# A two-block fp32 network on one core: the second block's attention loop reordered, and products of constants put in front of TensorE's waits

## The reference, cut to what matters

```python
for layer in range(DEPTH):                       # 2
    h = modulate(rmsnorm(x, norm_g[layer, 0]), sh1, sc1)
    x = x + 0.5 * g1 * swiglu_2(h, ...)          # feed-forward, FFN_C
    h = modulate(rmsnorm(x, norm_g[layer, 1]), sh2, sc2)
    proj = h @ w_in[layer]                       # the Z tiles
    (qa, ka, va, qb, kb, vb, qi, ki, wi, qc, kc, vc) = jnp.split(proj, ...)
    ...
    oa = moba_attention(qa, ka, ...)             # 4 heads, causal softmax here (256 tokens, one block)
    ob = dsa_attention(qb, kb, ..., qi, ki, wi)  # 4 heads, softmax over the picked keys
    oc = stick_breaking_attention(qc, kc, vc)    # 8 heads: logs, a running sum, an exponential
    o = rms_per_head(concat([oa, ob, oc])) * out_g[layer]
    x = x + g2 * (o @ w_out[layer])              # the Z_O tiles
    h = modulate(rmsnorm(x, norm_g[layer, 2]), sh3, sc3)
    x = x + 0.5 * g3 * swiglu_2(h, ...)          # feed-forward, FFN_D
```

## Time and profile before

| what | value |
| --- | --- |
| median of three runs | 2839.84 us (2837.78 to 2842.38) |
| the profiled execution, its own time | 2839.58 us |
| span from its first to its last instruction | 2837.5 us |
| PE busy | 2766.8 us, 98% of the span |
| DVE busy | 1951.3 us, 69% |
| ACT busy | 1366.8 us, 48% |
| mean granted TensorE clock | 0.992 |
| DMA | 564.42 MB, mean 199 GB/s |

### The profile page before, as it was taken

The page is one execution under the profiler, slowest core; times in us unless marked ns, Lnnn a source line. Parts: engine busy times, 40 slices in busy tenths (PEclk is TensorE's granted clock), DMA queues, the critical chain, the costliest instruction groups (busy, mean ns, idle before and its releaser), DMA issues.

```text
span 2837.5 us, 37822 instructions
## 1 busy us (share of the span) xinstructions
PE 2766.8 (98%) x16120; PEld 2426.8 (86%) x16120; DVE 1951.3 (69%) x2187; ACT 1366.8 (48%) x1562; POOL 228.7 (8%) x201
## 2 busy tenths in 40 slices
PE   8999999999999999999999999999899999999999
PEld 6889999998888889999998887878878878788787
DVE  6668876655666678877655667677876676677644
ACT  5444545455444445545454444444644444446433
POOL 0000420000000000520000000003000000030000
PEclk9999999999999999999999999999999999998999
DMA  8655433445766655333446666653266676442454
GB/s 306 257 220 183 149 125 136 164 164 210 263 261 248 248 208 189 138 136 132 171 165 228 257 255 243 260 218 134 90 244 251 239 274 253 177 150 95 176 189 148
DMA packets 82038, 564.42 MB, mean 199 GB/s; under 512 B 9072, under 2 KB 10576, under 8 KB 15952
## 3 DMA queue, kind: packets, MB, share of 16 engines
q1 hardware_dynamic: 66272, 465.47, 44.8%
q0 software_dynamic: 15600, 96.55, 9.0%
HBM read 560.86 MB, written 1.12 MB: 198 GB/s over the span
## 4 chain that ended last, share of the span: by engine, by line
PE 78%; DVE 13%; ACT 4%; POOL 2%; issue 2%; DMA 1%; SPq 0%; POOLq 0%; ACTq 0%; DVEq 0%
PE ps L332 71%; DVE ring_lo L327 4%; ACT w_hi L320 2%; POOL qk L2038 1%; PE ps L899 1%; POOL rope_a L2034 1%; DVE a_hg L1806 1%; DMA rows<-mod_rows 1%; DMA ring<-stream 1%; DVE e L1786 1%; DVE e L1785 1%; PE ps L1287 1%; DVE h_lo L576 0%; PE ps L1416 0%; PE ps L1442 0%
## 5 line engine op out<-in xcount | busy, mean ns | idle before, releaser
L327 DVE TENSOR_TENSOR ring_lo<-ring,w_hi 128x2048 fp32r<-128x2048 f32 x422 | 973.8, 2310 | 484.0 <-ACT w_hi L320 473.0
L320 ACT ACTIVATE w_hi<-ring 128x2048 fp32r<-128x2048 f32 x422 | 806.4, 1911 | 318.6 <-PE ps L332 188.0
L332 PE MATMUL ps<-w_hi,h_hi 128*128 128x512 f32 (+1 forms) x1920 | 728.9, 380 | 18.1 <-DVE ring_lo L327 9.0
L332 PE MATMUL ps<-w_hi,h_lo 128*128 128x512 f32 (+1 forms) x1920 | 717.0, 373 | 0.0
L332 PE MATMUL ps<-ring_lo,h_hi 128*128 128x512 f32 (+1 forms) x1920 | 716.3, 373 | 0.0
L332 PEld LDWEIGHTS ps<-w_hi,h_hi 128*128 128x128 f32 x1920 | 363.7, 189 | 85.6 <-DVE ring_lo L327 11.3
L332 PE MATMUL ps<-h_hi,w_hi 128*128 128x256 f32 x1488 | 431.6, 290 | 1.4 <-DVE h_lo L576 1.3
L332 PE MATMUL ps<-h_lo,w_hi 128*128 128x256 f32 x1488 | 423.0, 284 | 0.0
L332 PE MATMUL ps<-h_hi,ring_lo 128*128 128x256 f32 x1488 | 423.0, 284 | 0.0
L332 PEld LDWEIGHTS ps<-w_hi,h_lo 128*128 128x128 f32 x1920 | 363.2, 189 | 64.7
L332 PEld LDWEIGHTS ps<-ring_lo,h_hi 128*128 128x128 f32 x1920 | 363.8, 189 | 60.7 <-issue 1.0
(11 more groups left out here) (359 smaller groups left out, 3437.4 us busy)
## 6 DMA issues: line engine op xcount, KB each, us to landing
ring<-stream SPq DMA_DIRECT2D x438, 1024.0 KB, 4.8
e<-ada POOLq DMA_DIRECT2D x77, 1024.0 KB, 6.2
rows<-mod_rows POOLq DMA_DIRECT2D x18, 512.0 KB, 5.7
rows<-gain_rows POOLq DMA_DIRECT2D x8, 512.0 KB, 4.8
val<-c_row POOLq DMA_DIRECT2D x4, 512.0 KB, 5.3
x<-x_in SPq DMA_DIRECT2D x4, 256.0 KB, 6.7
mem<-mem_t SPq DMA_DIRECT2D x1, 1024.0 KB, 16.2
out_t<-x SPq DMA_DIRECT2D x4, 256.0 KB, 2.1
```

The lines of the kernel that those rows point to most:

```text
L320: nc.scalar.activation(hi_of(p), ring[:, p % RING, :], ACT.Copy).then_inc(S.w_hi_ready, 1)
L327: nc.vector.tensor_tensor(lo_of(p), ring[:, p % RING, :], hi_of(p).bitcast(F32), ALU.subtract).then_inc(S.w_lo_ready, 1)
L332: mm = nc.tensor.matmul(out, a, b, start=start and n == 0, stop=stop and n == 2, skip_group_check=group)
```

## The change

A new helper issues products of two constants into a bank of PSUM that nobody reads then. It is called ahead of waits of TensorE: in two levels of the first block, at the start of the first block's last feed-forward, at the start of both feed-forwards of the second block, around the transposes ahead of the Z tiles, and in the loop ahead of the last two transposes. It is called with 72 products in all.

The loop of the second block is written in another order. Tile 13 moves in front of the loop; the scores run two heads ahead and use other banks of PSUM; `turn_back` moves behind `weigh` on TensorE, `pair_high` behind `softplus` on ScalarE; and half of the first two output tiles' work (the new `out_ahead`, 12 products each time) moves from behind the loop into its last two rounds.

```diff
+        def hold_clock(bank, count):
+
+            for _ in range(count):
+                nc.tensor.matmul(ps[:, bank, :], ident, con_sb[:, 0:512], start=True, stop=True,
+                                 skip_group_check=True)
...
-        def first_three(pe, p, n, base, banks, done, turn_last):
+        def first_three(pe, p, n, base, banks, done, turn_last, hold):
             for b in range(2):
                 for k in range(KD):
                     if b == 0 and k % 4 == 0:
                         pe.wait_ge(S.w_lo_ready, p + k // 4 + 1)
+                    if k == 0:
+                        hold_clock(banks[b], hold[2 * b])
                     if k % 4 == 0:
                         pe.wait_ge(S.h_ready, nth(S.h_ready, 4 * n + 2 * b + k // 4 + 1))
...
                 if b == 0 and turn_last:
+                    hold_clock(banks[1], hold[1])
                     flip_x(pe, n, 1, base)
...
             def level(i):
+                if i in (2, 3):
+                    hold_clock(3, 2)
                 if i < LEVELS:
                     pe.wait_ge(S.e_ready, nth(S.e_ready, i + 1))
...
-            ffn_pe(pe, FFN_B, 1, 3, False, near=(lambda: flip_x(pe, 4, 0, 4)) if l < DEPTH - 1 else None)
+            ffn_pe(pe, FFN_B, 1, 3, False, near=(lambda: flip_x(pe, 4, 0, 4)) if l < DEPTH - 1 else None, hold=(2, 0, 0))
...
+        HOLD_FLIP, HOLD_SUMS = {6: 1, 7: 2}, {}
...
             if l == 0:
+                hold_clock(3, 7)
                 flip_x(pe, 0, 0, 4)
-            ffn_pe(pe, FFN_C, 0, 0, True, after=lambda: flip_x(pe, 1, 0, 4))
-
+
+            def z_flip():
+                hold_clock(3, 8)
+                flip_x(pe, 1, 0, 4)
+
+            ffn_pe(pe, FFN_C, 0, 0, True, after=z_flip, hold=(3, 0 if l == 0 else 1, 2))
+
+            hold_clock(3, 2)
             flip_x(pe, 1, 1, 4)
+            hold_clock(3, 2)
...
-            for n in range(9, 13):
+            for n in range(9, 14):
                 tile(n)
...
             def flip(n):
-                pe.wait_ge(S.exp_ready, nth(S.exp_ready, n + 1))
                 if n >= 1:
                     pe.wait_ge(S.pt_ready, nth(S.pt_ready, n))
+                hold_clock(6, HOLD_FLIP.get(n, 0))
+                pe.wait_ge(S.exp_ready, nth(S.exp_ready, n + 1))
...
-            scores_sticks(0)
-            for i in range(HEADS_2 + 2):
-                if i + 1 < HEADS_2:
-                    scores_sticks(i + 1)
-                if i in (0, 2):
-                    tile(13 + i // 2)
-                if 0 <= i - 1 < HEADS_2:
-                    flip(i - 1)
-                    sums(i - 1)
-                if i >= 5 and i % 2 == 1:
-                    turn_back((i - 5) // 2)
-                n = i - 2
-                if 0 <= n < HEADS_2:
-                    weigh(n, 0, n, pt2[:, n % 2, :], S.pt_ready, S.pv_done)
-                    weigh(n, 1, stick_head(n), st[:, 6 + n % 2, :], S.a_ready, S.o_done)
...
+            def out_ahead(pair):
+
+                pe.wait_ge(S.o_ready, nth(S.o_ready, pair + 1))
+                if pair == 0:
+                    pe.wait_ge(S.zm_ready, nth(S.zm_ready, HEADS_2))
+                pe.wait_ge(S.w_lo_ready, Z_O + 1)
+                for b in range(2):
+                    mm = out_part(0, 0, b, pair)
+                if pair == 1:
+                    mm.then_inc(S.tile_done, 1)
+
+            scores_sticks(0)
+            scores_sticks(1)
+            for i in range(HEADS_2 + 2):
+                n = i - 2
+                if i == 0:
+                    tile(14)
+                if 0 <= i - 1 < HEADS_2:
+                    flip(i - 1)
+                if i + 2 < HEADS_2 and i != 2:
+                    scores_sticks(i + 2)
+                if n >= HEADS_2 - 2:
+                    out_ahead(n - HEADS_2 + 2)
+                if 0 <= i - 1 < HEADS_2:
+                    sums(i - 1)
+                if 0 <= n < HEADS_2:
+                    weigh(n, 0, n, pt2[:, n % 2, :], S.pt_ready, S.pv_done)
+                    weigh(n, 1, stick_head(n), st[:, 6 + n % 2, :], S.a_ready, S.o_done)
+                if i >= 5 and i % 2 == 1:
+                    turn_back((i - 5) // 2)
+                if i == 2:
+                    scores_sticks(4)
...
-            ffn_pe(pe, FFN_D, 1, 2, True, after=(lambda: flip_x(pe, 3, 0, 4)) if l < DEPTH - 1 else None)
+            ffn_pe(pe, FFN_D, 1, 2, True, after=(lambda: flip_x(pe, 3, 0, 4)) if l < DEPTH - 1 else None,
+                   hold=(3, 1, 2))
...
+                if i == HEADS_2 + 3:
+                    next_high(act, Z_O)
                 if i >= 4 and i % 2 == 0:
                     pair_sq((i - 4) // 2)
+                if i < HEADS_2:
+                    softplus(i)
                 if i >= 5 and i % 2 == 1:
                     pair_high((i - 5) // 2)
-                if i < HEADS_2 and i != 3:
-                    softplus(i)
-                if i == 1:
-                    evac(13)
-            next_high(act, Z_O)
+                if i < 2:
+                    evac(13 + i)
```

More of the change, by code:

```diff
@@ L884, in out_ready, with ffn_pe @@
             return wait
-        def ffn_pe(pe, p0, f, n, shift, between=None, near=None, after=None):
+        def ffn_pe(pe, p0, f, n, shift, between=None, near=None, after=None, hold=(0, 0, 0)):
             def gate_up(i, half, p, b):
@@ L912, in down @@
                 return mm
-            first_three(pe, p0, n, 4, (0, 1), S.gu_done, shift)
+            first_three(pe, p0, n, 4, (0, 1), S.gu_done, shift, hold)
             if between:
@@ L2204, in unit_cols, with tile_bank @@
             return slice(i * n, (i + 1) * n)
+        def tile_bank(n):
+            return n % 3 if n < 13 else (3, 7)[n - 13]
         def two_pe(pe, l):
@@ L2390, in out_part @@
                 return mm
-            pe.wait_ge(S.o_ready, nth(S.o_ready, 2))
-            for c in range(2):
-                pe.wait_ge(S.w_lo_ready, Z_O + c + 1)
-                for pair in range(2):
-                    for b in range(2):
-                        mm = out_part(c, 0, b, pair)
-                mm.then_inc(S.tile_done, 1)
-                if c == 0:
-                    turn_back(3)
+            def out_ahead(pair):
[28 more added lines that the diff above has]
+                    scores_sticks(4)
+            pe.wait_ge(S.arg_ready, nth(S.arg_ready, HEADS_2))
+            pe.wait_ge(S.w_lo_ready, Z_O + 2)
+            for pair in range(2):
+                for b in range(2):
+                    mm = out_part(1, 0, b, pair)
+            mm.then_inc(S.tile_done, 1)
+            turn_back(3)
             pe.wait_ge(S.o_ready, nth(S.o_ready, 3))
@@ L2526, in two_act @@
             for i in range(HEADS_2 + 4):
-                if 0 <= i - 2 < HEADS_2 and i != 3:
+                if 0 <= i - 2 < HEADS_2:
                     flipped(i - 2)
@@ L2691, in stick @@
                 dve.wait_ge(S.z_done, nth(S.z_done, n + 1))
-                nc.vector.scalar_tensor_tensor(out=z_masked[n % 3], in0=ps[:, n % 2, 0:3 * P], scalar=HD ** -0.5,
+                nc.vector.scalar_tensor_tensor(out=z_masked[n % 3], in0=ps[:, 2 * (n % 2), 0:3 * P], scalar=HD ** -0.5,
                                                in1=C(C_M3, 3 * P), op0=ALU.mult,
@@ L2741, in two_dve @@
             chain(nc.vector.memset(stat[:, 0:32], 1.0))
-            for i in range(HEADS_2 + 4):
+            for i in range(HEADS_2 + 5):
                 if i < HEADS_2:
@@ L2745, in two_dve @@
                     stick(i)
-                if i == 3:
-                    low(dve, Z_V + 6 + HIGHS)
-                if i >= 5 and i % 2 == 1:
-                    pair_scaled((i - 5) // 2)
+                if 0 <= i - 1 < HEADS_2:
+                    stick_log(i - 1)
                 if 0 <= i - 2 < HEADS_2:
                     stick_arg(i - 2)
-                if 0 <= i - 1 < HEADS_2:
-                    stick_log(i - 1)
-                if i == 1:
-                    low(dve, Z_V + 5 + HIGHS)
-                if i == 5:
-                    low(dve, Z_V + 7 + HIGHS)
-                if i >= 4 and i % 2 == 0:
+                if i < 3:
+                    low(dve, Z_V + 5 + i + HIGHS)
+                if i >= 6 and i % 2 == 0:
+                    pair_low((i - 6) // 2)
+                if 5 <= i and i % 2 == 1:
+                    pair_scaled((i - 5) // 2)
+                if 4 <= i < HEADS_2 + 4 and i % 2 == 0:
                     pair_stat((i - 4) // 2)
-                if i >= 5 and i % 2 == 1:
-                    pair_low((i - 5) // 2)
+                if i == HEADS_2 + 3:
+                    low(dve, Z_O + HIGHS)
             def z_ready(q):
@@ L2772, in ahead @@
                     vectors_two(chain, l + 1)
-            low(dve, Z_O + HIGHS)
             shift_dve(dve, chain, 2, Z_O + 2, row_count + 6, 0, z_ready)
```

31 lines of the change are left out of this document (13 added, 18 removed).

## The result

The changed kernel takes 2847.6 us (median of seven runs, 2845.3 to 2850.3); the kernel before took 2837.9 beside it (seven runs, 2837.5 to 2843.2). The ratio is 1.0026 with a 95% interval of 1.0017 to 1.0036: slower, by 7.4 us by this ratio and by 9.7 between the two medians. The predicted time was 2842, its range 2833 to 2850; the likeliest side was no change, and the side that came is slower.

A forecast was written before the change was run, and what follows sets the result against it. TensorE, busy 98% of the span, was taken as the bound. The terms 1.1 + 0 + 1.4 + 1.0 + 0.4 + 4.8 - 1.3 - 5.3 gave +2.1 us on 2839.58, a median of 2842 us, range 2833 to 2850.

The forecast's parts named there:

- The price of a product: On TensorE: each fp32 product of constants takes two rows and 0.86 us, so the 72 are 62 us of new work.
- rival A: All places with products: a product is one row, 0.43 us, and fits everywhere; 2824 us, chance 0.08.
- Rival C: Second layer's last loop rounds: the clock still falls while TensorE waits; +8 us, 2848, chance 0.17.
- Rival D: First block's levels: their products are not swallowed, as the factors slip with TensorE; +6.9 us, 2849, chance 0.08.
- Ahead of the Z tiles: Second block, before the Z tiles: eight products and delayed transposes make them start later, +1.0 us first layer, +0.4 second.
- FFN_B: First block's last feed-forward: two products reach past the wait of 0.99 us; +1.1 us in two layers.
- the levels: First block: four products a layer, 3.4 us, fit the waits of the four levels after them; 0 us, bounds 0 and +6.9.
- the start of the second block: Products there exceed the waits, so the second half starts later although the clock stays up; +1.4 us.
- the feed-forward starts: FFN_D in both layers and FFN_C in the second: products exceed the waits, +1.6 us each, +4.8 together.
- The loops: Second block's loops: the new order saves 1.3 us in the first layer (bounds 0 and -5) and 5.3 in the second.
- Rival B: Second block's loops close up further, gaining 3.7 us a layer more; 2834.5 us, chance 0.17.
- The price of a stretch: Stretches at the lower clock lose half the time TensorE had work; the Z starts give back 2.5 and 3.1 us.

The follow-up runs named there:

- E3: The changed kernel with ScalarE's two squares of the second half's rows and their deviation put ahead of the first quarter's copy before the Z tiles: 2840.4 us, ratio 1.0003.
- E7: The changed kernel without its products in FFN_B, at both FFN_D starts and at the second layer's FFN_C start: 2842.0 us, ratio 1.0007.
- E11: E9 with four instead of two products ahead of levels 2 and 3: 2834.7 us, ratio 0.9973 to the kernel before.
- E4: The changed kernel with the eight products ahead of the Z tiles' first transposes replaced by four behind the first four transposes: 2835.1 us, ratio 0.9986.
- E10: E9 without the three products in each layer's loop: 2823.1 us, ratio 0.9936 to the kernel before.
- E1: The changed kernel with the reordered loop but no product of constants at all: 2832.2 us, ratio 0.9976 to the kernel before.
- E9: E5 with the changed kernel's products in the levels put back, two each ahead of levels 2 and 3: 2826.0 us, ratio 0.9941.
- E6: E5 without the three products in each layer's loop: 2830.3 us, ratio 0.9969 to the kernel before.
- E12: E9 without the eight products around the transposes ahead of the Z tiles in each layer: 2831.4 us, ratio 0.9971.
- E8: E5 without its seven products at the start of the second block: 2829.8 us, ratio 0.9965 to the kernel before.
- E5: E4 with fewer products at the second block's start and none in the levels, FFN_B and later feed-forward starts: 2827.6 us, ratio 0.9957.

## Why the prediction came out as it did

**The price of a product held.** All 144 rows of L339 are there, and sixteen take 6.86 us; rival A, with one row each, is out. The Trainium skill ("FP8 and Floating Point Precision", "TensorE Precision Notes") has four passes for true fp32, by which 0.86 was estimated, and the trace agrees.

That 2847.6 lies in the range is luck: the forecast's own range ended at 2846, and the wide range reaches to 2850 because of rivals C and D, whose mechanisms did not come (see below).

**The step that failed is "Ahead of the Z tiles"**, in its words "VectorE's low part of the first quarter now waits for transposes that the eight products hold back, and the second half's rows queue behind it, about 0.35 more". That named what is queued behind the late transposes on VectorE, and left out ScalarE, whose copy waits for the same transposes with the squares behind it. The 0.35 was a wait of 2.88, and the sum's +1.0 and +0.4 were +4.1 and +6.4. E3 shows the cause: with the squares and their deviation ahead of the copy and nothing else changed, the kernel is 6.5 us shorter by the two ratios. In the second layer's +6.4 the lower clock has a part: E3's profile takes back 5.6 there, against 2.7 in the first layer, where the clock was up in both, so by estimate 2.7 is the queue and 2.9 the clock. The sum had the clock up there and no term for a new wait. Of the marks set for the trace this one failed: a stretch at 0.50 remained.

**FFN_B, the levels, the start of the second block and the feed-forward starts** came near the sum, +1.0, 0, +1.5 and +4.2 where +1.1, 0, +1.4 and +4.8 stood. The terms listed for one feed-forward start add up to +2.0 (1.05 - 0.54 + 0.86 + 0.67), though, and not to the +1.6 that the sum took; measured were 1.6, 0.95 and 1.7. E7 took FFN_B and the later starts back at 4.9 where 5.3 had been measured. Rival D is out: E11 shows that the levels hold four products and not eight.

**The 0.99 behind the second block's start** was in no term. VectorE's low part waited for ScalarE's, and that for a weight tile still in transfer; E3's, E4's and E7's profiles, with the same seven products, don't have it. Why it came in one profile and not in others is open.

**The loops** won 2.1 and 6.2 where 1.3 and 5.3 were forecast, inside the bounds of the first. Rival B, 3.7 more a layer, is out. Rival C forecast 2848 and a clock that still falls; the time came, but not by its mechanism: in the changed kernel's profile the loops have no stretch at 0.50, and it was the Z start where the clock fell. E10 shows that C's mechanism exists once the loop's products are gone.

**What of the change earns its place.** The order of the loop does (E1). Of the products, those in the levels are free (E9) and steady the clock (E10 against E6; none of nine profiles with them has a stretch at the levels, three of five without have), those at the Z tiles are worth 2.3 to 2.4 a layer if they stand behind the first transposes (E12), those in the loop cost 1.4 and 1.8 in E6's profile, spared 2.0 and 2.3 in E10's, and by the medians are not paid back, those at the start of the second block, once cut to four, two and one, have no worth that was shown, and the rest only cost. E9 and E10 beat both kernels, by 0.6% against the kernel before.

**The price of a stretch** at the lower clock I took as half of TensorE's work in it behind the first product, 2.5 and 3.1 us at the two Z starts; E12 measured 2.3 and 2.4. The Trainium skill ("TensorE: Matmul & The Clock Gate", "HAM oscillation — how this bites in real kernels") reckons the penalty as the whole time at the lower clock times one half. By that rule alone the stretches in E12's two windows (10.9 us at a mean clock of 0.53, 10.2 at 0.51) would have cost an estimated 5.1 and 5.0; the traces do not agree: the Z tiles begin only in the middle of such a stretch (at 1918.34 in the earlier trace rows, of the stretch from 1913.03 to 1923.27 in the earlier trace rows), and ahead of that TensorE only makes transposes whose rows it waits for.

## What to carry to other kernels

Filler work in front of a wait is free only if nothing else waits for what stands behind the filler. List, for each engine that reads the delayed result, what is queued behind that reader; here the loss sat with the engine that the list left out. So put the filler behind the last instruction that another engine needs, and no more of it than the waits of this stretch hold. Measure a filler by taking it away place by place: in the sum, good and bad places cancel.

## What the runs showed of the hardware

Stretches at the lower clock come and go between executions of one kernel. With the same wait of 2.88 in both layers of the changed kernel the clock fell in one layer and not in the other. At the levels of the first block, whose waits are at most 1.1 us in each of these profiles, it fell in the profiles of E1, E6 and E8 and not in those of the kernel before and of E5, whose levels are the same. With it goes the spread: the kernel before took 2834.8 to 2844.0 in the runs beside E1 to E4, at mean clocks of 0.988 to 0.994, E9 2825.4 to 2827.5 at 0.999 to 1.000. A product that costs nothing can still buy a steadier time. The cost of a stretch isn't its length alone: one of 3.4 us cost 1.7 in E4's second loop and nothing in its first.
